# Splitting the layer input once and running its projections in three passes, with the weight splits between the convolution taps

## What is computed

```python
h = rms_norm(x, norm1_g[l])
u = h @ w_in[l]
(u_conv, c_q, c_kv, k_rope, hq, hf, hi, hg, u_gate) = jnp.split(u, SPLIT_POINTS, axis=-1)
y_a = conv_module(u_conv, ...)      # a * sigmoid(gt), 31-tap causal conv per channel, layer norm, silu, @ w_conv_out
y_b = mla(c_q, c_kv, k_rope, ...)   # latent attention, 8 heads
y_c = hgrn2(hq, hf, hi, hg, ...)    # gated linear recurrence, 4 heads
gates = jax.nn.sigmoid(u_gate).reshape(B, L, N_BRANCH, D)
mix = gates[:, :, 0] * y_a + gates[:, :, 1] * y_b + gates[:, :, 2] * y_c
x = x + mix @ w_out[l]
h2 = rms_norm(x, norm2_g[l])
x = x + jnp.square(jax.nn.relu(h2 @ w_ff1[l])) @ w_ff2[l]
```

## Time and profile before

| | us |
|---|---|
| median of 3 runs | 2810.4 |
| the runs | 2800.67 to 2823.55 |
| span of the profiled execution | 2818.1 |
| TensorE busy in it | 2674.3 (95%) |
| VectorE busy | 1717.9 (61%) |
| ScalarE busy | 1064.9 (38%) |
| GpSimd busy | 230.7 (8%) |

### The profile page before, as it was taken

The page is one execution under the profiler, slowest core; times in us unless marked ns, Lnnn a source line. Parts: engine busy times, 40 slices in busy tenths (PEclk is TensorE's granted clock), DMA queues, the critical chain, the costliest instruction groups (busy, mean ns, idle before and its releaser), DMA issues.

```text
span 2818.1 us, 50548 instructions
## 1 busy us (share of the span) xinstructions
PE 2674.3 (95%) x18768; PEld 2361.6 (84%) x18768; DVE 1717.9 (61%) x2943; ACT 1064.9 (38%) x1560; POOL 230.7 (8%) x225
## 2 busy tenths in 40 slices
PE   8999999999999989999889999999897899999997
PEld 6676678998675679997479999999884799999997
DVE  3663656545563656552566777777743657777776
ACT  1134333431234324433234444444344444444443
POOL 2631001004350001100000000000000000000000
PEclk9999899999998999999789999999998989999999
DMA  4331134543321235542124555555443245555553
GB/s 160 120 113 61 60 120 150 180 150 128 119 91 53 68 123 174 182 162 101 60 98 151 186 186 186 185 187 182 139 157 113 68 147 196 187 193 194 194 193 113
DMA packets 109772, 396.44 MB, mean 141 GB/s; under 512 B 12088, under 2 KB 14144, under 8 KB 109376
## 3 DMA queue, kind: packets, MB, share of 16 engines
q1 hardware_dynamic: 108576, 393.45, 42.3%
q10 hardware_dynamic: 1056, 1.06, 0.1%
HBM read 393.40 MB, written 1.06 MB: 140 GB/s over the span
## 4 chain that ended last, share of the span: by engine, by line
PE 84%; DVE 10%; ACT 4%; issue 2%; DMA 1%; DVEq 0%; ACTq 0%; SPq 0%
PE psum L489 83%; DVE region L1377 2%; DVE region L1380 1%; DVE RS L1409 1%; PE psum L497 1%; ACT region L1024 1%; DMA ring<-in_weights 1%; DVE region L1384 1%; DVE SQ L1377 1%; DVE W_LO L1372 1%; ACT SQ L1024 0%; ACT L1028 0%; ACT L1024 0%; DVE X_LO L1377 0%; ACT GATE L1024 0%
## 5 line engine op out<-in xcount | busy, mean ns | idle before, releaser
L1372 DVE TENSOR_TENSOR W_LO<-ring,W_HI 128x1024 fp32r<-128x1024 f32 x560 | 686.4, 1226 | 389.5 <-ACT W_HI L1019 358.8
L1019 ACT ACTIVATE W_HI<-ring 128x1024 fp32r<-128x1024 f32 x560 | 594.6, 1062 | 420.3 <-PE psum L489 300.3
L489 PE MATMUL psum<-X_HI,W_HI 128*128 128x256 f32 x2320 | 654.2, 282 | 8.5 <-DVE W_LO L1372 5.7
L489 PE MATMUL psum<-X_LO,W_HI 128*128 128x256 f32 x2320 | 651.3, 281 | 0.0
L489 PE MATMUL psum<-X_HI,W_LO 128*128 128x256 f32 x2320 | 651.3, 281 | 0.0
L489 PEld LDWEIGHTS psum<-X_HI,W_HI 128*128 128x128 f32 x2320 | 442.2, 191 | 12.7 <-issue 9.0
L489 PEld LDWEIGHTS psum<-X_HI,W_LO 128*128 128x128 f32 x2320 | 445.6, 192 | 0.0
L489 PEld LDWEIGHTS psum<-X_LO,W_HI 128*128 128x128 f32 x2320 | 441.8, 190 | 0.1
L489 PE MATMUL psum<-HN,ring 128*128 128x272 f32 x1600 | 389.4, 405 | 16.0 <-DVE HN L1384 16.0
L489 PEld LDWEIGHTS psum<-HN,ring 128*128 128x128 f32 x1600 | 309.9, 196 | 90.4 <-issue 24.8
L489 PE MATMUL psum<-HE_HI,W_HI 128*128 128x256 f32 x1024 | 285.2, 278 | 0.0
(11 more groups left out here) (221 smaller groups left out, 3724.4 us busy)
## 6 DMA issues: line engine op xcount, KB each, us to landing
ring<-in_weights SPq DMA_DIRECT2D x743, 512.0 KB, 3.3
XT<-in_x SPq DMA_DIRECT2D x1, 1088.0 KB, 5.0
CST<-in_consts SPq DMA_DIRECT2D x1, 1082.5 KB, 7.3
SQ<-bias_by_distance ACTq DMA_DIRECT2D x1, 1024.0 KB, 5.5
out<-XT SPq DMA_DIRECT2D x8, 128.0 KB, 1.9
PAR<-in_params SPq DMA_DIRECT2D x1, 572.0 KB, 8.2
bias_by_distance<-MIX ACTq DMA_DIRECT2D x1, 12.0 KB
```

The lines of the kernel that those rows point to most:

```text
L489: ins = nc.tensor.matmul(dst, w, x, start=start, stop=stop, skip_group_check=True)
L1019: lane(nc.scalar.activation(W_HI[:, s % SPLIT, :], ring[:, n % RING, :], ACT.Copy), split_hi)
L1372: lane(nc.vector.tensor_tensor(W_LO[:, s % SPLIT, :], ring[:, n % RING, :], W_HI[:, s % SPLIT, :].bitcast(F32), ALU.subtract), split_lo)
```

## The change

The layer input is split once, into `HN_HI` and `HN_LO`, after each first norm of a layer. All its projections and gates run split, apart from the first two of `conv_in` (`unsplit`) and the tokens of `hi`. The unsplit input moves into `SQ` and `MIX`. `conv_taps` on VectorE now calls `follow` after every third tap, with the keys of the projections in `begun`, so that `W_LO` steps stand among the taps. Four gates of branch 0 go ahead of `conv_norm`. `reached` counts a chunk as used only once its release has been issued.

```diff
@@ conv_in, hgrn_in, on TensorE
-            hn = lambda k: HN[:, k, :]
+            hn = lambda k: (HN_HI[:, k, :], HN_LO[:, k, :])
+            unsplit = lambda r: lambda k: HN[r % 2][:, k, :]
                 for j in range(4):
-                    project(("conv_a", l, j), hn, ready=None if j else till("normed", KT * 2 * l))
-                    project(("conv_g", l, j), hn)
+                    lead = unsplit(2 * l)
+                    project(("conv_a", l, j), hn if j else lead, ready=(till("normed", KT * 2 * l), till("norm_split", KT * 2 * l))[j] if j < 2 else None)
+                    project(("conv_g", l, j), hn if j else lead)
@@
-                tokens(("hi", l), lambda k, lo, n: HN[:, k, lo : lo + n], TOK1)
+                tokens(("hi", l), lambda k, lo, n: HN[0][:, k, lo : lo + n], TOK1)
@@ norm and conv_taps, on VectorE
+                else:
+                    for k in range(KT):
+                        split_tile(HN_HI[:, k, :], HN_LO[:, k, :], HN[0][:, k, :], sem("norm_split"))
@@
+                begun = [(n, l, j) for n in ("hf", "hq", "hg") for j in range(4)] + [("cq", l, 0), ("cq", l, 1), ("ckv", l), ("rope", l)]
+                begun += [("gate", l, 0, m) for m in range(4)]
                 for j in range(3):
                     for i in range(CONV_K):
                         x, w, b = tap(l, j, i)
+                        if begun and i % 3 == 0:
+                            follow(begun.pop(0))
@@ schedule
-        s += [("conv_in", l), ("conv_taps", l), ("hgrn_in", l), ("mla_in", l), ("conv_norm", l)]
-        s += [("gate", l, 0, 0), ("conv_var", l), ("mla_norm", l), ("hgrn_prep", l)]
-        s += [("gate", l, 0, m) for m in range(1, KT)] + [("hgrn_clamp", l, 0), ("hgrn_clamp", l, 1), ("hgrn_args", l, 0)]
+        s += [("conv_in", l), ("conv_taps", l), ("hgrn_in", l), ("mla_in", l)] + [("gate", l, 0, m) for m in range(4)]
+        s += [("conv_norm", l), ("gate", l, 0, 4), ("conv_var", l), ("mla_norm", l), ("hgrn_prep", l)]
+        s += [("gate", l, 0, m) for m in range(5, KT)] + [("hgrn_clamp", l, 0), ("hgrn_clamp", l, 1), ("hgrn_args", l, 0)]
```

More of the change, by code:

```diff
@@ L362, in build_program @@
         with ExitStack() as phase:
-            HN = sb("HN", KT, T, stack=phase)
+            HN_HI = sb("HN_HI", KT, T, dtype=F32R, stack=phase)
             GATES = [sb("GATE0", KT, T, stack=phase), GATE1]
+            with ExitStack() as before_bias:
+                HN_LO = sb("HN_LO", KT, T, dtype=F32R, stack=before_bias)
             BIAS_C = sb("BIAS_C", HEADS, 256, stack=phase)
@@ L449, in build_program @@
         CHID = BC
+        HN = [SQ[:, : KT * T].rearrange("p (k t) -> p k t", k=KT), MIX[:, :, :]]
         def par(name, rows=128):
@@ L476, in _, with reached @@
             keys = {}
+            def reached():
+                late = state["release"]
+                return len(splits.chunks) - sum(s is split_used for s in late), state["n"] - len(late)
             def filled(done):
-                splits.marks[keys.pop(done.name)] = (len(splits.chunks), state["n"])
+                splits.marks[keys.pop(done.name)] = reached()
             def mm(dst, w, x, start=True, stop=True, done=None):
@@ L539, in tokens @@
                     w = chunk(isinstance(x(0, 0, 128), tuple))
-                    splits.marks[(*key, "chunks")] = (len(splits.chunks), state["n"])
+                    splits.marks[(*key, "chunks")] = reached()
                     for i, (lo, n) in enumerate(tiles):
@@ L734, in ff1 @@
                 for m in range(FH * half, FH * half + FH):
-                    project(("ff1", l, m), (lambda k: (FN_HI[:, k, :], FN_LO[:, k, :])) if m > 1 else hn,
-                            ready=(till("normed", KT * (2 * l + 1)), None, till("norm_split", KT * l))[m] if m < 3 else None)
+                    project(("ff1", l, m), (lambda k: (FN_HI[:, k, :], FN_LO[:, k, :])) if m > 1 else unsplit(1),
+                            ready=(till("normed", KT * (2 * l + 1)), None, till("norm_split", KT * (2 * l + 1)))[m] if m < 3 else None)
             def ff2(l, half):
@@ L991, in _ @@
                     steps[name](*args)
-                splits.marks["step", name, *args] = (len(splits.chunks), state["n"])
+                splits.marks["step", name, *args] = reached()
             splits.known = frozenset(splits.chunks)
@@ L1452, in norm @@
                 for k in range(KT):
-                    stt(HN[:, k, :], XT[:, k, :], g[:, k : k + 1], RS[:, :T], ALU.mult, ALU.mult, sem("normed"))
+                    stt(HN[r % 2][:, k, :], XT[:, k, :], g[:, k : k + 1], RS[:, :T], ALU.mult, ALU.mult, sem("normed"))
                 if r % 2:
                     for k in range(KT):
-                        split_tile(FN_HI[:, k, :], FN_LO[:, k, :], HN[:, k, :], sem("norm_split"))
+                        split_tile(FN_HI[:, k, :], FN_LO[:, k, :], HN[1][:, k, :], sem("norm_split"))
+                else:
+                    for k in range(KT):
+                        split_tile(HN_HI[:, k, :], HN_LO[:, k, :], HN[0][:, k, :], sem("norm_split"))
                 if r == 2:
```

## The result

The changed kernel takes **2920.5 us** (median of four, 2912.4 to 2935.2) against 2817.0 us for the kernel before beside it: a ratio of **1.040, interval 1.034 to 1.045**. Slower was the likeliest case; the size, 2881 and at most 2912, was too small. The interval is a loss of 97 to 126 us. The profiled execution of the changed kernel spans 2910.4 us, that of the kernel before 2818.1.

The account below looks back on a forecast made before the run. TensorE, carrying 84% of the chain, was taken as the bound, with any wait before it counting. First layer +41.1 and second +29.8 gave +71 us on 2810.4, so 2881 us, range 2838 to 2912.

Parts of the forecast that it names:

- The bound and the sign: TensorE carries 84% of the chain, so waits put before it always count; slower result given 0.81.
- the stand at the column sums: Before the conv norm's column sums TensorE waits 23.2 us in the first layer for VectorE's last 38 taps.
- A: Whole kernel: TensorE leads throughout and runs faster, -38 us, giving 2772 us; chance 0.09.
- B: Conv taps: they are not held and only the rest of the sum stands, +24.6 us, 2835 us; chance 0.09.
- Term 1: Lead-in before `hf`: waits for splits make it start 12.6 us later in the first layer, 1.3 in the second.
- Term 2: Conv taps with splits between: taps held, TensorE waits 23.2 us; including the lead-in +39.9 us, second layer +28.6.
- the slip: `hq` and `hg`: VectorE's three taps and a W_LO lag TensorE over eight chunks, 2 us, bounds 0 and 9.
- Term 3: After the column sums' wait: lower TensorE clock +2.5 us, gates brought forward -5.0 us.
- Term 4: hgrn blocks: five W_LO between mask and clamp add 1.4 us each, +7 us (6 to 12); gates are fillers.
- The sign that I had named: hgrn blocks: their period becomes 1.3 to 1.5 us longer if the prediction is right.
- Term 5: Third gate branch to the end of the blocks: cheaper gates give -3.3 us, between -6.5 and +4.
- Rival C: Taps and blocks: W_LO waits for GpSimd, up to 1.03 us more each in the taps, 2911 us; chance 0.12.

Follow-up runs that it names:

- Experiment 5: Changed kernel with the six conv projections that the change split run unsplit again; 2903.5 us, ratio 1.033 to the kernel before.
- Experiment 4: Changed kernel with gates 0 to 3 of branch 0 moved back behind the conv norm's column sums; 2949.3 us, ratio 1.050 to the kernel before.
- Experiment 3: Changed kernel with the eight branch 1 gates in the hgrn blocks unsplit, read from HN_HI alone; 2881.4 us, ratio 1.026 to the kernel before.
- experiment 2: Changed kernel with VectorE giving W_LO after the clamp in the first seven hgrn blocks; 2922.9 us, ratio 1.037 to the kernel before.
- experiment 9: Changed kernel with the branch 1 gate put ahead of each hgrn block's scores on every engine; 2904.3 us, ratio 1.037 to the kernel before.
- experiment 11: Kernel before with only the four latent projections and eight branch 2 gates of each layer split; 2803.9 us, ratio 0.999 to the kernel before.
- 7: Changed kernel with conv, hf, hq, hg unsplit, no W_LO among taps, W_LO after the clamp in the blocks; 2839.1 us, ratio 1.011 to the kernel before.

## Why the prediction was right or wrong

**The bound and the sign** were right: a wait put in front of TensorE counts, and the stand at the column sums came at the named place with the named length (7.09 and 15.31 us, 22.4 together for 23.2, and 38 taps behind the last W_LO). Rivals A and B did not occur; the taps are held, 16.23 us.

**Term 1, the lead-in** (+12.6, measured +16.9; +1.3 in the second layer, measured +4.2): the waits were right (7.2 and three of 2.4 to 2.5). The six split projections between them took 22.0 us and not 18.1, at a clock of 0.86. I had priced them at 3.02 us, a row at full clock, though the waits that I had just put between them lower it. The second layer has the same three waits of 2.5 us, which its +1.3 had counted; its clock was 0.95. Experiment 5 confirms the term.

**Term 2** had the right mechanism at the decisive place and was 3.8 us short in each layer: +31.1 for +27.3 from `hf` to the mean, in both. Of the 3.8 us, 2.2 are the slip, which I took at 2 out of bounds of 0 and 9: the twelve projections took 40.5 us and not 36.2, because a W_LO beside GpSimd took 1.40 or 1.69, and three taps with it 3.70 on average and not 3.34.

**Term 3** was right in its sum: -2.6 for -2.5 in both layers; its two parts, +2.5 and -5.0, were not measured apart. Experiment 4 shows that the moved gates were worth 24 us of that stretch, and 30 us at the end of the first block, which I had not seen: I had costed the move, not what would have happened without it.

**Term 4, the hgrn blocks, is the step that failed**: +7 (6 to 12) per layer, measured +18.3 and +17.8. The prediction counted W_LO's own duration and took the gates for "fillers here". But W_LO waits for W_HI, W_HI stands behind ScalarE's read of the gate, and the gate is TensorE's, so placing W_LO between mask and clamp closed a ring TensorE, ScalarE, VectorE, ScalarE, VectorE. Experiment 3 (no split in the blocks) removes all of it in the first layer and all but 0.9 us in the second, experiment 2 (W_LO and clamp out of the ring) 7 us, experiment 9 (the gate early enough) 13 to 15 in the blocks and 8 to 11 net. The sign that I had named, a period 1.3 to 1.5 us longer, did not come: every second period was 0.5 to 1.2 us shorter than before and the others 3.9 to 6.3 us longer. The term also had nothing for the clock; TensorE's two pieces above give it some 4 us a round. The question that I put at the taps ("what does the W_HI stand behind?") I did not put here.

**Term 5, the third branch** (-3.3 per layer): +4.4 and -2.0 between the last copy and the next layer or the end of the block. The gain was not there in the first layer; experiment 11 does not settle it, since the first of these stretches varied by 8 us without a change of its code.

**Rival C, contention**, was the nearest in time (2911), but not by its mechanism. Among the taps beside GpSimd a W_LO took 1.40 and 1.69 us in turn against 1.23, so +0.17 and +0.46 and not +1.03, some 2.5 us in eight. The Trainium skill (SBUF — State Buffer, Who interferes with whom) has an exclusive lock for a whole instruction between such a pair; the trace agrees that they get in each other's way. What a W_LO lost was less than half of one GpSimd instruction of 1.03 us, and GpSimd lost too: its instruction at 101.84 us, begun during a W_LO, took 1.81. That fits a wait for the rest of an instruction already running; my rival C had charged each W_LO with a whole one.

Over the first block the 117 us are 83 from the stretches up to the mean (48.0 and 35.3: lead-in, hold, late last split), 36 from the blocks and -3 from the rest; the conv splits are behind 18 of the 83 (experiment 5).

## What to carry to other kernels

Splitting weights on two other engines turns a projection that TensorE could do whenever its chunk was there into one that needs two instructions from in-order queues; for each one ask what its W_HI and its W_LO stand behind, and what stands behind them, in every stage and not only where the diff shows it. If one of these is a read of TensorE's own result and the other is ahead of TensorE's next input, a filler has become a link of the loop. A projection that is 18% cheaper pays only where TensorE leads and the splitting engines have time: here that was shown for four projections of 46 per layer, worth 1 us in each layer, and it is too little to show in the time of the kernel.

## What the runs showed of the hardware

**One code, two speeds, at full clock.** Each of the two mixture-of-experts loops of the second block runs at one of two rates, and keeps it for the whole loop. The kernel before, in its first loop and in its second:

```profile
1700.00:1770.00 70.00, 70.00 (x596) 70.00 (x596) 50.83 (x76) 28.98 (x33) 0.00 (x0) 1.00 0.58 187
...
2500.00:2570.00 70.00, 70.00 (x620) 70.00 (x619) 52.26 (x78) 31.01 (x35) 0.00 (x0) 1.00 0.58 190
```

TensorE is never idle in either, the clock is 1.00 in both, and yet there are 596 or 620 matmuls in 70 us (281 or 276 ns each in the groups). Of the thirteen profiled executions here one had the slow rate in the first loop (the kernel before) and three in the second (experiments 2, 7 and 11); their second blocks took 1564.5 to 1570.8 us, the others 1544.1 to 1553.8. So some 20 us of a run depend on it, which is most of the -24.3 in the first table and could be most of the spread of each kernel's times (24 to 36 us between the runs of the kernel before in one comparison). What sets the rate stays open.

**The clock falls with the waits.** In the blocks of the first layer the granted clock was 1.00 without splits, 0.88 with the gate ahead, 0.83 with W_LO after the clamp and 0.76 in the changed kernel, in the order of their lengths. These are means over stretches in which TensorE is now at 2.4 and now at 1.2 GHz, as the two windows of 0.51 and 1.00 in the section on the result show.

**The clamp beside GpSimd.** In the blocks of the changed kernel the clamp of 1024 columns takes 0.69 us, and 2.34 while GpSimd shifts arguments:

```profile
248.17 2.34 DVE L1391 TENSOR_SCALAR region<-region 128x1024 f32<-128x1024 f32 x1
```

```profile
247.49 2.46 POOL L1958 TENSOR_TENSOR SQ<-region 128x1024 f32<-128x1024 f32 x1 [3.44 <-PE psum L498]
```

The 1.65 us that this clamp lost are more than the W_LO of 1.23 us which pushed it there. But it is the only one: the six clamps between first and last copy take 5.8 us together in the changed kernel and 7.3 in the kernel before, where five of them take 0.97 to 1.69 (one is the 1.16 of the earlier trace rows). So the clamps have no part in the 18 us. In experiment 9 they take 10.0, five of them 1.78 to 2.00; these 2.7 us more than before are half of what that order leaves over 47.9 in the first layer.
